# A transformer kernel on one core: where a feed-forward's down-projection tiles stand in the stream of weights

## The chip, the cores and the metric

The kernel runs on one core of one Trainium2 chip. The metric is the device time of one execution in microseconds (us). TensorE does the matrix products, VectorE and ScalarE the elementwise work, GpSimd (POOL) a few tiny operations, and SyncE (SP) issues the DMAs.

## What is computed

Two blocks of two layers each run on a sequence of 256 tokens with 1024 channels, in fp32: a convolution layer and an attention layer, each with a feed-forward, and then a retention layer and a sparse-attention layer. The change touches the feed-forward alone, which stands behind each layer of the first block:

```python
def conv_ffn(h, w_up, w_dw, b_dw, w_down):
    u = h @ w_up                       # (256, 1024) @ (1024, 5632)
    u = causal_dwconv(u, w_dw, b_dw)   # three taps over tokens, per channel
    gate, val = jnp.split(u, 2, axis=-1)
    return (jax.nn.silu(gate) * val) @ w_down   # (256, 2816) @ (2816, 1024)

x = x + conv_ffn(rmsnorm(x, g_ffn[l]), w_up[l], w_dw_f[l], b_dw_f[l], w_down[l])
```

## The kernel before

**Weights as a stream of tiles.** All weights pass through the core once, as a stream of tiles of 128 x 2048 fp32 (1 MB), in the order that `plan_tiles` writes down. For each tile SP loads RAW, ScalarE rounds it to a high part WH (L1216), VectorE subtracts to get the low part WL (L1595, called the split here), and TensorE multiplies. A product is three passes: high by high, low by high, high by low (L710 to L712). RAW, WH and WL each hold three tiles (`RING`). ScalarE rounds tile t when it is loaded and TensorE is done with tile t - 3 (`w_used`); SP loads into RAW when tile t - 3 is split.

**The order on each engine is written out by hand.** Each engine runs its instructions in the order of its own program. On ScalarE and VectorE, `upto_n(n)` stands where rounds and splits are to go: it rounds or splits all tiles up to number n + 2 that are not yet done.

**A feed-forward** (`ffn`) has 11 steps (`FSTEP`). Step s has a gate tile `("fg", l, s)` and a value tile `("fv", l, s)`, each of 256 hidden channels, and, `LAG` = 2 steps later, a down tile `("fd", l, s)` that multiplies the finished product of step s into four banks that hold the residual's increment. Steps 0 and 1 have no down tile. Behind step 10 the down tiles of steps 9 and 10 follow alone. A gate or value tile is 48 matmuls with 256 columns, a down tile 24 with 512. Between the entry of the feed-forward and its end the work of a step is:

- VectorE scales the gate tile out of its bank (L1656), and splits one tile (L1595). ScalarE applies the bias and the middle tap (L1323, twice), VectorE the other two (L1728 and L1732, twice each).
- ScalarE takes the tanh of the gate (L1327) and rounds the next tile (L1216).
- VectorE scales the value tile (L1656), splits a tile, finishes the sigmoid (L1724), and, behind ScalarE's L1323, applies the taps to the value (L1728, L1732).
- VectorE multiplies gate and value (L1736, called the product). From step 2 to step 9 a third tile is rounded (behind ScalarE's value part) and split (behind L1736).
- ScalarE copies the product to its high part MH (L1332), VectorE subtracts to get the low part ML (L1741). TensorE's down tile waits for this (`lo_done`).

Behind the last down tile VectorE adds the four banks to x (L1611), TensorE transposes x (L844), ScalarE squares it for the next norm (L1234) and writes the next layer's activations (L1248), VectorE their low part (L1624).

`plan_banks` writes down which PSUM bank each product uses and who gives it back; ring A has four banks for gate and value tiles, ring B four for the transposes and the down tiles.

Of the kernel before, what the change touches and what calls it, by code (L numbers as in the profile page):

```python
# [62 lines left out]
def plan_tiles():  # L63

    t = []
    for j in range(3):
        t += [("ca", j), ("cg", j)]
    t += [("qm", 0)]
    for l in range(2):
        t += [("mk", l), ("mv", l)]  # L70
    t += [("o0", c) for c in O0_ORDER]

    def ffn(l):
        out = []
        for s in range(FSTEP):
            out += [("fg", l, s), ("fv", l, s)] + [("fd", l, s - LAG)] * (s >= LAG)
        return out + [("fd", l, s) for s in range(FSTEP - LAG, FSTEP)]

    t += ffn(0)
    t += FOX_FIRST + FOX_LATER + [("o1", c) for c in range(4)]  # L80
    t += ffn(1)
    for h in range(RH):
        t += [("rq", h), ("rk", h)]
    for h in range(RH):
        t += [("rv", h, 0), ("rv", h, 1), ("rg", h, 0), ("rg", h, 1)]
    t += [("ro", c) for c in range(8)]
    t += [("pe", 0)] + [("pg0", c) for c in range(4)]
    for n in ("kc", "vc", "ks", "kw"):
        t += [(n, j) for j in range(2)]
    for n in ("vs", "vw"):  # L90
        t += [(n, j) for j in range(2)]
    t += [(n, j) for n in ("c1k", "c1v") for j in CMP_ORDER]
    for j in range(8):
        t += [("nq", j), ("ng", j)]
    t += [("no", c) for c in range(8)]
    t += [("pe", 1)] + [("pg1", c) for c in range(4)]
    return t
# [25 lines left out]
def plan_banks():  # L123
# [53 lines left out]
    def ffn(l, n):  # L177
        enter(n, ("fg", l, 0), ("fv", l, 0))
        for s in range(1, FSTEP):
            gemm(("fg", l, s), "dve")  # L180
            gemm(("fv", l, s), "dve")
            if s == LAG:
                acc(f"f{l}", ("fd", l, FSTEP - 1))

    gemm(("ca", 0), "dve")
    gemm(("cg", 0), "dve")
# [143 lines left out]
def program(nc, wstream, params, consts, ident_in, x_in, mem_in, xT_in, memT_in, p_in, b_f, g_final, final_norm, out):  # L330
    NT = len(TILES)
    with ExitStack() as ctx:
# [349 lines left out]
        def _(pe):  # L682
# [256 lines left out]
            def ffn(l, n, n_next):  # L939
                enter(n, (("fg", l, 0), XH, XL), (("fv", l, 0), XH, XL))  # L940
                for s in range(1, FSTEP + LAG):
                    if s < FSTEP:
                        gemm_t(("fg", l, s), XH, XL)
                        gemm_t(("fv", l, s), XH, XL)
                    if s == LAG:
                        o = [take((f"f{l}", q)) for q in range(4)]
                    if s >= LAG:
                        d = s - LAG
                        pe.wait_ge(*lo_a.next())
                        if d < FSTEP - 1:  # L950
                            gemm_d(("fd", l, d), o, MH, ML, 2 * (d % 4), d == 0)
                        else:
                            gemm_d_last(("fd", l, d), o, MH, ML, 2 * (d % 4), None, n_next)

            def ple(l):
                n = 7 + 2 * l
# [246 lines left out]
        def _(act):  # L1203
# [109 lines left out]

            def ffn(l):
                for s in range(FSTEP):
                    e, at = s % 2, TILE[("fg", l, s)]
                    for q, name in enumerate(("fg", "fv")):
                        upto_n(at + 1 + q)
                        is_free(act, (name, l, s))
                        for b in range(2):  # L1320
                            f = q * 22 + 2 * s + b
                            c = slice((2 * q + b) * T, (2 * q + b + 1) * T)
                            act_fn(fy[:, e, c], fu[:, e, c], ACT.Identity, bias=col(f"b_dw_f{l}", f),  # L1323
                                   scale=col(f"w_dw_f{l}", 2 * 44 + f)).then_inc(act_for_dve, 1)
                        if q == 0:
                            act.wait_ge(*dve_a.next())
                            act_fn(fth[:, e, :], fy[:, e, 0:2 * T], ACT.Tanh, scale=0.5).then_inc(act_for_dve, 1)  # L1327
                    if LAG <= s < FSTEP - 1:
                        upto_n(at + 3)
                    act.wait_ge(*dve_a.next())  # L1330
                    m = 2 * (s % 4)
                    act_fn(MH[:, m:m + 2, :], fa[:, e, :].rearrange("p (b t) -> p b t", b=2), ACT.Copy).then_inc(hi_done, 1)  # L1332
                    if s == FSTEP - 1:
                        upto_n(at + 3)

            def ple(l, key):
                n = 7 + 2 * l
# [245 lines left out]
        def _(dve):  # L1583
# [128 lines left out]

            def ffn(l):
                for s in range(FSTEP):
                    e, at = s % 2, TILE[("fg", l, s)]
                    y = fy[:, e, :].rearrange("p (b t) -> p b t", b=4)
                    u = fu[:, e, :].rearrange("p (b t) -> p b t", b=4)
                    for q, name in enumerate(("fg", "fv")):
                        scaled((name, l, s), u[:, 2 * q:2 * q + 2, :])
                        upto_n(at + 1 + q)  # L1720
                        is_free(dve, (name, l, s))
                        if q == 1:
                            dve.wait_ge(*act_a.next())
# [9 lines left out]
                        sync()  # L1733
                        if q == 0:
                            dve.drain().then_inc(dve_for_act, 1)
                    stt(fa[:, e, :], fth[:, e, :], 0.5, fy[:, e, 2 * T:4 * T], ALU.mult, ALU.mult).then_inc(dve_for_act, 1)  # L1736
                    if LAG <= s < FSTEP - 1:
                        upto_n(at + 3)
                    dve.wait_ge(*hi_a.next())
                    m = 2 * (s % 4)  # L1740
                    tt(ML[:, m:m + 2, :], fa[:, e, :].rearrange("p (b t) -> p b t", b=2),  # L1741
                       MH[:, m:m + 2, :].bitcast(F32), ALU.subtract).then_inc(lo_done, 1)
                    if s == FSTEP - 1:
                        upto_n(at + 3)

            def ple(l, acc, key):
                n = 7 + 2 * l
# [589 lines left out]
```

## Time and profile before

| | |
|---|---|
| median of 3 runs | 1295.65 us (1293.98 to 1296.0) |
| profiled execution | 1293.94 us, its span 1292.0 us |
| granted TensorE clock, mean | 0.985 |
| TensorE matmuls busy | 1244.0 us (96%) |
| TensorE weight loads busy | 1112.0 us (86%) |
| VectorE busy | 889.9 us (69%) |
| ScalarE busy | 640.1 us (50%) |
| POOL busy | 12.4 us (1%) |
| DMA | 200.54 MB, 155 GB/s |
| splits L1595 | 180, 2289 ns each |
| rounds L1216 | 180, 1910 ns each |

Busy time overlaps between engines, and that of TensorE is modelled from the starts of pipelined matmuls. A matmul's row is longer than the distance to the next one's start, so distances between starts are what to count with. The same holds for rows on VectorE and ScalarE, by some 0.1 us each. In a row, the part in square brackets is how long the engine stood idle before it and what ended that.

### The profile page before, as it was taken

What the parts mean: (1) busy time and instruction counts of PE and PEld (TensorE: products, weight loads), DVE (VectorE), ACT (ScalarE), POOL (GpSimd) and SP (SyncE); (2) the same over time, 40 slices, a digit from 0 to 9 for tenths busy, and PEclk for the clock granted to TensorE, in tenths of its full rate; (3) what the DMA queues carried; (4) which work ended last, traced back from release to release, by engine and by line L of the source; (5) the groups of instructions that cost most, each with busy time, mean ns of one, the idle gap of its engine ahead of it and who ended that gap; (6) DMA issues with size and microseconds to landing.
All of it is one profiled execution on the core that took longest, in us unless ns stands there. A gap on an engine that the chain in (4) does not pass through costs nothing.

```text
span 1292.0 us, 19500 instructions
## 1 busy us (share of the span) xinstructions
PE 1244.0 (96%) x8068; PEld 1112.0 (86%) x8068; DVE 889.9 (69%) x1358; ACT 640.1 (50%) x1015; POOL 12.4 (1%) x28
## 2 busy tenths in 40 slices
PE   6999899999999999999999999899899999999996
PEld 6988798999898769899999987687798989999885
DVE  5995678877755557887779666645485656666664
ACT  6563645555534335555555344425534545555453
POOL 0000000000000000000000000000000000000000
PEclk9999999999989999999999999999899899999998
DMA  9610445555342223455545544443355632222341
GB/s 387 233 66 5 160 166 193 199 193 188 139 155 106 99 98 131 156 211 188 195 164 176 191 155 185 165 160 131 133 196 195 228 109 97 98 99 98 130 169 60
DMA packets 28567, 200.54 MB, mean 155 GB/s; under 512 B 3392, under 2 KB 3520, under 8 KB 4928
## 3 DMA queue, kind: packets, MB, share of 16 engines
q1 hardware_dynamic: 28480, 199.30, 42.2%
q8 instruction: 64, 1.05, 0.3%
q14 instruction: 23, 0.19, 0.0%
HBM read 198.24 MB, written 1.05 MB: 154 GB/s over the span
## 4 chain that ended last, share of the span: by engine, by line
PE 82%; DVE 8%; issue 5%; ACT 4%; DMA 0%; DVEq 0%; POOL 0%; POOLq 0%; ACTq 0%; SPq 0%
PE bank L710 23%; PE bank L712 22%; PE bank L711 22%; PE bank L858 3%; DVE WL L1595 3%; ACT WH L1216 3%; PE bank L1190 1%; PE bank L1165 1%; PE bank L922 1%; PE bank L1156 1%; PE bank L1173 1%; PE bank L1188 1%; DVE work L1732 1%; DVE work L1728 1%; PE bank L914 1%
## 5 line engine op out<-in xcount | busy, mean ns | idle before, releaser
L1595 DVE TENSOR_TENSOR WL<-RAW,WH 128x2048 fp32r<-128x2048 f32 x180 | 411.6, 2289 | 173.7 <-ACT WH L1216 172.9
L1216 ACT ACTIVATE WH<-RAW 128x2048 fp32r<-128x2048 f32 x180 | 343.2, 1910 | 225.2 <-PE bank L712 221.7
L710 PE MATMUL bank<-XH,WH 128*128 128x256 f32 x1264 | 361.6, 286 | 17.9 <-DVE WL L1799 11.8
L711 PE MATMUL bank<-XL,WH 128*128 128x256 f32 x1264 | 358.2, 283 | 0.0
L712 PE MATMUL bank<-XH,WL 128*128 128x256 f32 x1264 | 358.0, 283 | 0.0
L710 PEld LDWEIGHTS bank<-XH,WH 128*128 128x128 f32 x1264 | 242.9, 192 | 22.4 <-DVE XL L1792 11.8
L711 PEld LDWEIGHTS bank<-XL,WH 128*128 128x128 f32 x1264 | 243.1, 192 | 0.5
L712 PEld LDWEIGHTS bank<-XH,WL 128*128 128x128 f32 x1264 | 243.0, 192 | 0.0
L710 PE MATMUL bank<-WH,MH 128*128 128x512 f32 (+1 forms) x544 | 202.5, 372 | 10.6 <-DVE work L2037 4.0
L712 PE MATMUL bank<-WH,ML 128*128 128x512 f32 (+1 forms) x544 | 199.9, 368 | 0.0
L711 PE MATMUL bank<-WL,MH 128*128 128x512 f32 (+1 forms) x544 | 199.8, 367 | 0.0
L710 PEld LDWEIGHTS bank<-WH,MH 128*128 128x128 f32 x544 | 105.9, 195 | 29.1 <-issue 5.6
L712 PEld LDWEIGHTS bank<-WH,ML 128*128 128x128 f32 x544 | 105.3, 194 | 16.3
L711 PEld LDWEIGHTS bank<-WL,MH 128*128 128x128 f32 x544 | 105.9, 195 | 14.6
L710 PE MATMUL bank<-WH,XH 128*128 128x512 f32 x192 | 76.3, 398 | 0.0
L711 PE MATMUL bank<-WL,XH 128*128 128x512 f32 x192 | 74.8, 390 | 0.0
L712 PE MATMUL bank<-WH,XL 128*128 128x512 f32 x192 | 74.7, 389 | 0.0
L710 PE MATMUL bank<-MH,WH 128*128 128x256 f32 x208 | 61.0, 293 | 4.4 <-DVE ML L1624 3.7
L1560 ACT ACTIVATE work<-bank,stat,rs_n 128x128 f32<-128x128 f32 (+1 forms) x96 | 42.9, 461 | 34.3 <-DVE stat L2153 34.3
L711 PE MATMUL bank<-ML,WH 128*128 128x256 f32 x208 | 59.7, 287 | 0.0
L712 PE MATMUL bank<-MH,WL 128*128 128x256 f32 x208 | 59.7, 287 | 0.0
L1323 ACT ACTIVATE work<-work,par 128x256 f32<-128x256 f32 x88 | 47.5, 587 | 4.8 <-DVE work L1656 4.8
(256 smaller groups left out, 1557.7 us busy)
## 6 DMA issues: line engine op xcount, KB each, us to landing
RAW<-wstream SPq DMA_DIRECT2D x181, 1024.0 KB, 4.8
con<-consts SPq DMA_DIRECT2D x1, 1681.0 KB, 13.5
work<-xT_in SPq DMA_DIRECT2D x1, 1024.0 KB, 4.8
x<-x_in SPq DMA_DIRECT2D x1, 1024.0 KB, 11.0
work<-mem_in SPq DMA_DIRECT2D x1, 1024.0 KB, 15.9
xn<-memT_in SPq DMA_DIRECT2D x1, 1024.0 KB, 13.7
out_dram<-xn SPq DMA_DIRECT2D x2, 512.0 KB, 2.7
par<-params SPq DMA_DIRECT2D x1, 858.0 KB, 14.2
```

Of the source, the lines that this page charges most:

```text
L710: mm(o, ah, bh, start=start, stop=False)
L711: mm(o, ah, bl, start=False, stop=False)
L712: return mm(o, al, bh, start=False, stop=stop)
L858: mm(conv_out[b][:, 0:T], diag[:, n % DIAGS, :], vpad[:, b, k:k + T], start=(k == 0), stop=last)\
L914: last = mm(o[:, i * T:(i + 1) * T], q_mem[r, h // 2, i * P:(i + 1) * P], mkt[r, l, h // 2, :], start=True, stop=True)
L922: mm(o[:, a:a + n], q1[r, h // 2, t], k1[r, h // 2, 0:n], start=True, stop=False)
L1156: mm(oS[:, a:a + n], qh[:, i * P:(i + 1) * P], ksT[:, g, 0:n], start=True, stop=False)
L1165: mm(oW[:, a:a + n], qh[:, i * P:(i + 1) * P], kwT[:, g, 0:n], start=True, stop=False)
L1216: act_fn(WH[:, t % RING, :], RAW[:, t % RING, :], ACT.Copy).then_inc(w_rounded, 1)
L1323: act_fn(fy[:, e, c], fu[:, e, c], ACT.Identity, bias=col(f"b_dw_f{l}", f), scale=col(f"w_dw_f{l}", 2 * 44 + f)).then_inc(act_for_dve, 1)
L1560: ins = act_fn(dst[:, e, b:b + w], B((name, s))[:, a:a + w], ACT.Exp, bias=stat[:, c:c + 1], scale=rs_n[:, i:i + 1], accum_out=stat[:, 16 ...
L1595: tt(WL[:, t % RING, :], RAW[:, t % RING, :], WH[:, t % RING, :].bitcast(F32), ALU.subtract).then_inc(w_split, 1)
```

## The change

In steps 2 to 9 the down tile moves from behind the value tile to a place between the gate and the value tile. Step 10 keeps the old order, and steps 0 and 1 have no down tile. The stream's order, the banks' plan, TensorE's program, and the places of the rounds and splits on ScalarE and VectorE all change with it: the round that stood behind ScalarE's value part now stands ahead of it, and on VectorE one split moves ahead of the scaling of the value and one behind it, ahead of the value's taps.

```diff
@@ plan_tiles
-            out += [("fg", l, s), ("fv", l, s)] + [("fd", l, s - LAG)] * (s >= LAG)
+            down = [("fd", l, s - LAG)] * (s >= LAG)
+            out += [("fg", l, s)] + (down + [("fv", l, s)] if s < FSTEP - 1 else [("fv", l, s)] + down)
@@ TensorE, ffn
                     if s < FSTEP:
                         gemm_t(("fg", l, s), XH, XL)
+                    if s == FSTEP - 1:
                         gemm_t(("fv", l, s), XH, XL)
...
                             gemm_d_last(("fd", l, d), o, MH, ML, 2 * (d % 4), None, n_next)
+                    if s < FSTEP - 1:
+                        gemm_t(("fv", l, s), XH, XL)
@@ ScalarE, ffn
                     for q, name in enumerate(("fg", "fv")):
-                        upto_n(at + 1 + q)
+                        upto_n(TILE[(name, l, s)] + 1)
...
                             act_fn(fth[:, e, :], fy[:, e, 0:2 * T], ACT.Tanh, scale=0.5).then_inc(act_for_dve, 1)
-                    if LAG <= s < FSTEP - 1:
-                        upto_n(at + 3)
+                            if LAG <= s < FSTEP - 1:
+                                upto_n(TILE[("fd", l, s - LAG)] + 1)
                     act.wait_ge(*dve_a.next())
@@ VectorE, ffn
                         scaled((name, l, s), u[:, 2 * q:2 * q + 2, :])
-                        upto_n(at + 1 + q)
+                        upto_n(TILE[(name, l, s)] + 1)
...
                         if q == 0:
                             dve.drain().then_inc(dve_for_act, 1)
+                            if LAG <= s < FSTEP - 1:
+                                upto_n(TILE[("fd", l, s - LAG)] + 1)
                     stt(fa[:, e, :], fth[:, e, :], 0.5, fy[:, e, 2 * T:4 * T], ALU.mult, ALU.mult).then_inc(dve_for_act, 1)
-                    if LAG <= s < FSTEP - 1:
-                        upto_n(at + 3)
                     dve.wait_ge(*hi_a.next())
```

The line numbers below L72 move by one to four in the changed kernel (the split L1595 becomes L1599, the product L1736 becomes L1742, the low part L1741 becomes L1745, the round L1216 becomes L1220).

VectorE, one step of the first feed-forward from the scaling of the gate to the low part, before:

```order
L1656 TENSOR_TENSOR work<-bank,rb 128x512
L1595 TENSOR_TENSOR WL<-RAW,WH 128x2048
L1728 SCALAR_TENSOR_TENSOR work<-work,par 128x255 x2
L1732 SCALAR_TENSOR_TENSOR work<-work,par 128x254 x2
L1656 TENSOR_TENSOR work<-bank,rb 128x512
L1595 TENSOR_TENSOR WL<-RAW,WH 128x2048
L1724 SCALAR_TENSOR_TENSOR work<-work 128x512
L1728 SCALAR_TENSOR_TENSOR work<-work,par 128x255 x2
L1732 SCALAR_TENSOR_TENSOR work<-work,par 128x254 x2
L1736 SCALAR_TENSOR_TENSOR work<-work 128x512
L1595 TENSOR_TENSOR WL<-RAW,WH 128x2048
L1741 TENSOR_TENSOR ML<-work,MH 128x512
```

VectorE, the same step of the changed kernel:

```order
L1660 TENSOR_TENSOR work<-bank,rb 128x512
L1599 TENSOR_TENSOR WL<-RAW,WH 128x2048
L1732 SCALAR_TENSOR_TENSOR work<-work,par 128x255 x2
L1736 SCALAR_TENSOR_TENSOR work<-work,par 128x254 x2
L1599 TENSOR_TENSOR WL<-RAW,WH 128x2048
L1660 TENSOR_TENSOR work<-bank,rb 128x512
L1599 TENSOR_TENSOR WL<-RAW,WH 128x2048
L1728 SCALAR_TENSOR_TENSOR work<-work 128x512
L1732 SCALAR_TENSOR_TENSOR work<-work,par 128x255 x2
L1736 SCALAR_TENSOR_TENSOR work<-work,par 128x254 x2
L1742 SCALAR_TENSOR_TENSOR work<-work 128x512
L1745 TENSOR_TENSOR ML<-work,MH 128x512
```

The second split went ahead of the scaling of the value, and the third from behind the product to behind that scaling; the product and the low part now follow each other.

ScalarE, one step of the first feed-forward from the round ahead of the gate's part to the high part, before:

```order
L1216 ACTIVATE WH<-RAW 128x2048
L1323 ACTIVATE work<-work,par 128x256 x2
L1327 ACTIVATE work<-work 128x512
L1216 ACTIVATE WH<-RAW 128x2048
L1323 ACTIVATE work<-work,par 128x256 x2
L1216 ACTIVATE WH<-RAW 128x2048
L1332 ACTIVATE MH<-work 128x512
```

ScalarE, the same step of the changed kernel:

```order
L1220 ACTIVATE WH<-RAW 128x2048
L1327 ACTIVATE work<-work,par 128x256 x2
L1331 ACTIVATE work<-work 128x512
L1220 ACTIVATE WH<-RAW 128x2048 x2
L1327 ACTIVATE work<-work,par 128x256 x2
L1336 ACTIVATE MH<-work 128x512
```

Both later rounds now stand in a row behind the tanh, ahead of the value's bias and middle tap.

## Rows read from the trace of the kernel before

**Rows 1.** Busy time by stretch: us long, then busy us of each engine (and instructions), PEclk, DMA share, GB/s.

```profile
217.84:302.74 84.90, 84.90 (x601) 80.11 (x600) 69.07 (x82) 46.64 (x48) 0.00 (x0) 1.00 0.54 193
```

**Rows 2.** Waits from 158 to 345 us: us in total, times, longest.

```profile
PE bank L710 <- DVE WL L1595: 2.0, 2, 1.4
```

**Rows 3.** Timeline, TensorE, first feed-forward: start, us, instruction, idle before.

```profile
200.01 0.36 PE L710 MATMUL bank<-XH,WH 128*128 128x256 f32 x1 [1.40 <-DVE WL L1595]
...
206.56 0.36 PE L710 MATMUL bank<-XH,WH 128*128 128x256 f32 x1 [0.56 <-DVE WL L1595]
...
212.38 0.40 PE L710 MATMUL bank<-WH,MH 128*128 128x512 f32 x1
...
217.84 0.28 PE L710 MATMUL bank<-XH,WH 128*128 128x256 f32 x1
...
234.82 0.28 PE L710 MATMUL bank<-XH,WH 128*128 128x256 f32 x1
...
342.14 0.39 PE L710 MATMUL bank<-WH,MH 128*128 128x512 f32 x1
```

**Rows 4.** Timeline, VectorE, steps 2 and 3 of the first feed-forward.

```profile
204.12 2.29 DVE L1595 TENSOR_TENSOR WL<-RAW,WH 128x2048 fp32r<-128x2048 f32 x1 [1.72 <-ACT WH L1216]
206.33 0.69 DVE L1724 SCALAR_TENSOR_TENSOR work<-work 128x512 f32<-128x512 f32 x1
206.93 0.88 DVE L1728 SCALAR_TENSOR_TENSOR work<-work,par 128x255 f32<-128x255 f32 x2
...
208.75 0.69 DVE L1736 SCALAR_TENSOR_TENSOR work<-work 128x512 f32<-128x512 f32 x1
209.36 2.28 DVE L1595 TENSOR_TENSOR WL<-RAW,WH 128x2048 fp32r<-128x2048 f32 x1
...
212.17 0.68 DVE L1656 TENSOR_TENSOR work<-bank,rb 128x512 f32<-128x512 f32 x1
212.77 2.28 DVE L1595 TENSOR_TENSOR WL<-RAW,WH 128x2048 fp32r<-128x2048 f32 x1
214.97 0.87 DVE L1728 SCALAR_TENSOR_TENSOR work<-work,par 128x255 f32<-128x255 f32 x2
...
219.30 2.29 DVE L1595 TENSOR_TENSOR WL<-RAW,WH 128x2048 fp32r<-128x2048 f32 x1 [1.72 <-ACT WH L1216]
```

**Rows 5.** Timeline, ScalarE, the same steps.

```profile
209.48 0.63 ACT L1332 ACTIVATE MH<-work 128x512 fp32r<-128x512 f32 x1 [2.60 <-DVE work L1736]
210.02 1.90 ACT L1216 ACTIVATE WH<-RAW 128x2048 fp32r<-128x2048 f32 x1
...
216.83 0.63 ACT L1327 ACTIVATE work<-work 128x512 f32<-128x512 f32 x1 [2.85 <-DVEq L1735]
217.37 1.90 ACT L1216 ACTIVATE WH<-RAW 128x2048 fp32r<-128x2048 f32 x1
```

**Rows 6.** Timeline, VectorE, last low part of both feed-forwards and what follows.

```profile
340.25 0.69 DVE L1741 TENSOR_TENSOR ML<-work,MH 128x512 fp32r<-128x512 f32 x1 [0.70 <-ACT MH L1332]
342.06 2.29 DVE L1595 TENSOR_TENSOR WL<-RAW,WH 128x2048 fp32r<-128x2048 f32 x1 [1.11 <-ACT WH L1216]
344.27 1.48 DVE L1611 TENSOR_TENSOR x<-bank,x 128x512 f32<-128x512 f32 x2
...
674.21 0.69 DVE L1741 TENSOR_TENSOR ML<-work,MH 128x512 fp32r<-128x512 f32 x1 [0.70 <-ACT MH L1332]
```

**Rows 7.** TensorE behind two long pauses, and the stretch behind each (columns as rows 1).

```profile
139.45 0.47 PE L710 MATMUL bank<-WH,MH 128*128 128x512 f32 x1 [3.13 <-DVE WL L1595]
139.45:143.00 3.55, 3.55 (x16) 2.94 (x17) 3.45 (x9) 1.85 (x2) 0.00 (x0) 1.00 0.67 240
...
840.31 0.47 PE L710 MATMUL bank<-WH,MH 128*128 128x512 f32 x1 [4.03 <-DVE work L2037]
...
840.30:844.60 4.30, 4.29 (x12) 3.43 (x13) 3.39 (x3) 0.00 (x0) 0.00 (x0) 0.60 0.00 0
```

**Rows 8.** DMA issues of the page: engine, operation, count, KB each, us to landing.

```profile
RAW<-wstream SPq DMA_DIRECT2D x181, 1024.0 KB, 4.8
```

More of the change, by code:

```diff
@@ L180, in ffn @@
             gemm(("fg", l, s), "dve")
-            gemm(("fv", l, s), "dve")
             if s == LAG:
                 acc(f"f{l}", ("fd", l, FSTEP - 1))
+            gemm(("fv", l, s), "dve")
     gemm(("ca", 0), "dve")
@@ L1315, in ffn @@
                 for s in range(FSTEP):
-                    e, at = s % 2, TILE[("fg", l, s)]
+                    e = s % 2
                     for q, name in enumerate(("fg", "fv")):
-                        upto_n(at + 1 + q)
+                        upto_n(TILE[(name, l, s)] + 1)
                         is_free(act, (name, l, s))
@@ L1714, in ffn @@
                 for s in range(FSTEP):
-                    e, at = s % 2, TILE[("fg", l, s)]
+                    e = s % 2
                     y = fy[:, e, :].rearrange("p (b t) -> p b t", b=4)
@@ L1735, in ffn @@
                             dve.drain().then_inc(dve_for_act, 1)
+                            if LAG <= s < FSTEP - 1:
+                                upto_n(TILE[("fd", l, s - LAG)] + 1)
                     stt(fa[:, e, :], fth[:, e, :], 0.5, fy[:, e, 2 * T:4 * T], ALU.mult, ALU.mult).then_inc(dve_for_act, 1)
-                    if LAG <= s < FSTEP - 1:
-                        upto_n(at + 3)
                     dve.wait_ge(*hi_a.next())
@@ L1743, in ffn @@
                     if s == FSTEP - 1:
-                        upto_n(at + 3)
+                        upto_n(TILE[("fd", l, s - LAG)] + 1)
             def ple(l, acc, key):
```

## The prediction

> **What bounds the kernel now.** I read the page first, then the busy time by stretch inside one feed-forward, then the waits there, and at last the instructions of single steps on TensorE, VectorE and ScalarE. Both feed-forwards give the same rows 334 us apart (340.25 and 674.21 for the last low part [rows 6]), so one is worked out and counted twice. The page's shares are means over a dozen stages and decide nothing here; the stretch does.
>
> In five full steps of the first feed-forward TensorE is busy for all of 84.90 us, its weight loads for 80.11, VectorE for 69.07 and ScalarE for 46.64 [rows 1]. The start of the gate tile of step 4 and that of step 5 are 16.98 us apart [rows 3]: that is TensorE's step, gate, value and down tile back to back, the down tile with 5.46 of it (212.38 to 217.84) and the other two with 5.76 each. So from there on TensorE bounds. Before that it does not quite: it waits twice for a split weight, 2.0 us together [rows 2], 1.40 before the gate tile of step 3 and 0.56 before its value tile [rows 3]. Steps 0 and 1 have no down tile, TensorE goes through them faster than the other two engines, and these come out of step 2 late.
>
> The question is how long the round that VectorE and ScalarE hand to each other takes. In the steps just after the start they are late and run as fast as they can. From the split at 204.12 to its counterpart at 219.30 it takes 15.18 us [rows 4]. That is 1.80 below TensorE's 16.98, so they make up their lateness step by step, and afterwards wait for TensorE. Some reserve of this sort is what the order of work in a step must keep.
>
> **What the change does to that round.** Nothing is added or removed: per step the same three splits (2.2 us each), rounds (1.9), taps and products, and on SP the same loads of 1 MB. A load lands 4.8 us after its issue [rows 8] and is issued when the tile three before it has been split. Even where splits now stand closest, one scaling apart, the copy in the ring that is filled next was freed a whole step earlier than it is rounded, so loads stay hidden. If that cover were gone, the price would be a part of 4.8 us a step. POOL does nothing in these stretches. The banks of the gate and value tiles are given back by scalings two steps back, which is no limit.
>
> What moves is the third split of a step. Before, it stands behind the product L1736, and while VectorE does it (from 209.36, 2.28 long), ScalarE copies the product (209.48) and rounds the next step's first tile (210.02 on) [rows 4, 5]. When VectorE has done the split, the low part and a scaling, that rounded tile is ready, and VectorE splits at 212.77 without a wait. In the changed order the third split stands between the scaling of the value and the value's taps, on the path to the product; and behind the product there is nothing left but the low part and a scaling, so that VectorE must wait for ScalarE's copy and round. The second split too stands ahead of the scaling instead of behind it, and the scaling no longer fills VectorE's wait for the tanh and the round behind it.
>
> The new round from product to product, each hand-over from a row [rows 4, 5]: product to ScalarE's copy 0.73 (208.75 to 209.48); to the round 0.54 (210.02); round to split 1.93 (217.37 to 219.30); split to taps 2.20 (212.77 to 214.97); through both pairs of taps to the tanh 1.86 (216.83); to the round 0.54 (217.37); to the split of the down tile 1.93 (219.30); to the scaling of the value 2.21 (as 204.12 to 206.33); to the split of the value tile's place 0.60; to L1724 2.21; to the value's taps 0.60; to the product 1.82 (206.93 to 208.75). **The sum is 17.17 us**, against 15.18 now and against TensorE's 16.98. The two engines can no longer catch up: they stay as late as they were at step 2, and lose another 0.19 a step.
>
> **When the last product is there.** Up to the split at 204.12 nothing changes: the first two steps have the same order, the tile that holds TensorE up at 200.01 is still the eighth of the stream, and its split stands where it stood. The second wait, at 206.56, falls to the down tile that now has this place. So the gain at these two waits is nothing. Then, in step 2, scaling, split, L1724, taps and product follow: 204.12 + 2.21 + 0.60 + 2.21 + 0.60 + 1.82 = 211.56 for the product, where it was at 208.75. Seven rounds of 17.17 bring the product of step 9 to 331.75. The last step has its old order, with no third split: 0.73 + 0.54 + 1.93 + 2.20 + 1.86 + 0.54 + 1.93 + 2.21 + 0.60 + 1.82 = 14.36, product at 346.11. Its high part (0.73 later, 0.63 long) and its low part (0.03 behind it, 0.69 long [rows 6]) are done at 348.19, and TensorE starts 0.15 behind what it waits for (split 204.12 + 2.29, start 206.56 [rows 3, 4]). So **the last down tile starts at 348.34**. It starts at 342.14 now [rows 3], with 1.2 us in hand behind the low part of 340.25 + 0.69 [rows 6]. The loss at this place is 6.20 us in each feed-forward. It shows as some 0.2 us of waiting at each of seven or eight down tiles, and as one pause of 5 us at the end: the product of step 8 is at 314.58, the split of step 10's value tile, the second of step 9, starts 9.73 behind it at 324.31 and TensorE on it at 326.75; 5.76 for it and 5.46 for each of two down tiles end at 343.4, 4.9 us before 348.34.
>
> **Behind the last down tile.** Now the split at 342.06 lies 1.81 behind the low part, since the round comes behind the high part, and VectorE's first residual add is at 344.27, 2.13 behind the start of the down tile [rows 6, 3]. Late by the new chain, low part at 347.50, split at 349.31, add at 351.51: 3.17 behind the tile's start. The second add ends at about 352.8, 4.46 behind it. The transposes that wait for it stand behind three quarters of the tile, 4.09 behind its start. So they slip by 0.5, ScalarE's squares by 1.0, and what feeds the next product by about 0.7. Bounds for this term: 0, if the later waits of that entry take it up, and 1.0.
>
> The pause costs more where the clock reacts. After a pause of 4.03 us at 840.31 the granted clock of the next 4.3 us was 0.60 of full, which is a part at 1.2 GHz among 2.4 [rows 7]; at 0.5 while halved, 0.60 over 4.30 us is 3.4 us at the lower level, and it costs half of that, 1.7 us. After a pause of 3.13 us at 139.45 the clock stayed at full [rows 7]. A pause of 5 us is nearer to the first, so I take 1.7; with TensorE slower, the second add is in time for the transposes, and the 0.7 is not counted beside it. The bounds are 0 and twice 1.7. The Trainium skill, TensorE: Matmul & The Clock Gate, What's actually happening, says that the throttled state is the default and that activity releases it; the trace agrees at 840.31, and by the rule alone any such pause is a risk of its own, beside the wait itself.
>
> **The sum.** 6.20 + 1.7 = 7.9 us per feed-forward, 15.8 for two. On the profiled execution's 1293.94 that is 1309.7; its time lies 1.7 under the median of the runs, 1295.65, and for the median I get **1311.5 us**.
>
> **Rivals.**
> (a) The same chain, but no loss of clock: 6.20 + 0.7 twice is 13.8, 1309.5 us. For it speaks the pause of 3.13 without one.
> (b) The round comes out shorter than TensorE's 16.98, because a hand-over overlaps that I put in a row (a second round behind the first is back to back on ScalarE, say). At 16.5 the two engines gain 0.5 a step and the last product is 8 times 0.67 = 5.4 earlier than in my chain; 2 times 0.8 and no clock loss, some 2 to 8 us in all, 1298 to 1304. Against it: each hand-over has its row, and the same way of adding gives exactly 15.18 for the present order.
> (c) No change, 1295.65: VectorE is busy 69.07 of 84.90 and has 16 us to spare [rows 1], TensorE stays full, and the lateness hides in the ring. The Trainium skill, Perfetto Trace Analysis, Identifying the Most-Contended Engine, has one look for the engine of the highest occupancy, weight loads for TensorE, and improve that; by it TensorE stays the bound and an order that leaves its work alone changes nothing. The trace agrees that TensorE is the fullest in this stretch. Against it: the limit here is a round through two engines, and it is 17.17 however idle each is.
> (d) Faster. The down tile of step 0, put ahead of the value tile, gives VectorE and ScalarE 5.5 us before the value is asked for, and the two waits of 1.40 and 0.56 go in both feed-forwards: 3.9 us, 1291.7. It decides itself at one point: whether the split of step 3's gate tile is done by 198.6, when TensorE comes to it. Against it: the same three tiles stand ahead of it on TensorE, and VectorE's order up to it is the same.
>
> **How the numbers follow.** My forecast has 0.60, (a) 0.25, (b) 0.06, (c) 0.05, (d) 0.04. The range: below, (a) without the 0.7 is 1308.1, and an error of 0.1 in the round (8 rounds, twice, 1.6) gives 1306.5; I go to 1304.5 to take in the nearest of (b). Above, another 1.7 of lost clock twice is 1314.9, and with 1.6 for the round 1316.5. So 1304.5 to 1317. A measurement of this kernel can tell about 0.2%, 2.6 us, from no change; faster by more than that is (d), 0.04; within it (c), 0.05; slower 0.91.
>
> **What would show it.** Right: a period of about 17.2 us between gate tiles; VectorE idle behind each low part, waiting for a round, and again ahead of the second split; splits of the second and third place one scaling apart; TensorE's wait for the low part (L1745) before the last down tile of each feed-forward, near 5 us, and two stretches of lower clock behind it. Wrong: a period of 16.98 with TensorE full, or the last down tile less than 3 us later than 342.14; then a term of the round overlaps. If the wait is there but the clock stays, (a) holds. If loads (L596) appear among what ScalarE's rounds wait for, my cover for the DMAs was wrong.

## The result

| | before | changed |
|---|---|---|
| median | 1295.66 us (4 runs, 1293.98 to 1296.0) | 1313.54 us (4 runs, 1312.47 to 1314.59) |
| ratio to before | | 1.0137 (95% interval 1.0122 to 1.0152) |
| span of the profiled execution | 1292.0 us | 1310.6 us |
| mean granted clock | 0.985 | 0.980 |

The changed kernel is slower by 17.9 us between the medians and by 18.6 between the profiled spans. The forecast was 1311.5 in a range of 1304.5 to 1317.

From the page of the changed kernel, the busy times of the engines (with instructions) and the shares of the chain that ended last:

```profile
PE 1253.2 (96%) x8068; PEld 1116.5 (85%) x8068; DVE 889.5 (68%) x1358; ACT 638.2 (49%) x1015; POOL 12.4 (1%) x28
...
PE 61%; DVE 21%; ACT 9%; issue 8%; DMA 0%; DVEq 0%; POOL 0%; ACTq 0%; POOLq 0%; SPq 0%
```

The shares of busy time tell nothing of it: VectorE and ScalarE do the same work in the same time. The chain does. Of the span before, 82% went over TensorE and 8% over VectorE; now it is 61% and 21%.

### The profile page after: what moved, and what is told of

It reads as the page before. It is cut to its first block, busy times and chain, and to the rows that moved or that the text cites. A ratio compares the mean times of both kernels' runs of the same rounds, so it can differ in the third digit from the quotient of the medians.

```text
span 1310.6 us, 19500 instructions
## 1 busy us (share of the span) xinstructions
PE 1253.2 (96%) x8068; PEld 1116.5 (85%) x8068; DVE 889.5 (68%) x1358; ACT 638.2 (49%) x1015; POOL 12.4 (1%) x28
## 4 chain that ended last, share of the span: by engine, by line
PE 61%; DVE 21%; ACT 9%; issue 8%; DMA 0%; DVEq 0%; POOL 0%; ACTq 0%; POOLq 0%; SPq 0%
PE bank L711 15%; PE bank L712 15%; PE bank L713 15%; DVE WL L1599 8%; ACT WH L1220 7%; DVE work L1736 3%; DVE work L1732 3%; PE bank L859 3%; PE bank L1194 1%; DVE work L1742 1%; DVE work L1660 1%; DVE work L1728 1%; PE bank L1169 1%; PE bank L923 1%; PE bank L1160 1%
## 5 line engine op out<-in xcount | busy, mean ns | idle before, releaser
L1599 DVE TENSOR_TENSOR WL<-RAW,WH 128x2048 fp32r<-128x2048 f32 x180 | 411.6, 2289 | 183.6 <-ACT WH L1220 182.8
L1220 ACT ACTIVATE WH<-RAW 128x2048 fp32r<-128x2048 f32 x180 | 341.0, 1908 | 183.8 <-PE bank L713 180.2
L711 PE MATMUL bank<-WH,MH 128*128 128x512 f32 (+1 forms) x544 | 206.8, 380 | 20.9 <-DVE ML L1745 9.2
L1336 ACT ACTIVATE MH<-work 128x512 fp32r<-128x512 f32 x22 | 13.9, 632 | 92.5 <-DVE work L1742 92.5
```

Source lines behind the costliest of these rows:

```text
L711: mm(o, ah, bh, start=start, stop=False)
L1220: act_fn(WH[:, t % RING, :], RAW[:, t % RING, :], ACT.Copy).then_inc(w_rounded, 1)
L1599: tt(WL[:, t % RING, :], RAW[:, t % RING, :], WH[:, t % RING, :].bitcast(F32), ALU.subtract).then_inc(w_split, 1)
```

## The profile after

**The round.** VectorE in steps 2 and 3 of the first feed-forward, the counterpart of [rows 4] (start, us, instruction, idle before):

```profile
204.32 2.29 DVE L1599 TENSOR_TENSOR WL<-RAW,WH 128x2048 fp32r<-128x2048 f32 x1 [2.55 <-ACT WH L1220]
206.53 0.68 DVE L1660 TENSOR_TENSOR work<-bank,rb 128x512 f32<-128x512 f32 x1
207.13 2.28 DVE L1599 TENSOR_TENSOR WL<-RAW,WH 128x2048 fp32r<-128x2048 f32 x1
209.33 0.68 DVE L1728 SCALAR_TENSOR_TENSOR work<-work 128x512 f32<-128x512 f32 x1
...
211.76 0.69 DVE L1742 SCALAR_TENSOR_TENSOR work<-work 128x512 f32<-128x512 f32 x1
213.15 0.69 DVE L1745 TENSOR_TENSOR ML<-work,MH 128x512 fp32r<-128x512 f32 x1 [0.70 <-ACT MH L1336]
213.75 0.68 DVE L1660 TENSOR_TENSOR work<-bank,rb 128x512 f32<-128x512 f32 x1
214.95 2.29 DVE L1599 TENSOR_TENSOR WL<-RAW,WH 128x2048 fp32r<-128x2048 f32 x1 [0.52 <-ACT WH L1220]
...
221.50 2.29 DVE L1599 TENSOR_TENSOR WL<-RAW,WH 128x2048 fp32r<-128x2048 f32 x1 [2.55 <-ACT WH L1220]
...
228.93 0.69 DVE L1742 SCALAR_TENSOR_TENSOR work<-work 128x512 f32<-128x512 f32 x1
```

ScalarE in the same steps, the counterpart of [rows 5]:

```profile
202.39 3.70 ACT L1220 ACTIVATE WH<-RAW 128x2048 fp32r<-128x2048 f32 x2
...
212.48 0.63 ACT L1336 ACTIVATE MH<-work 128x512 fp32r<-128x512 f32 x1 [4.13 <-DVE work L1742]
213.02 1.90 ACT L1220 ACTIVATE WH<-RAW 128x2048 fp32r<-128x2048 f32 x1
```

From product to product it is 228.93 - 211.76 = 17.17 us, which is the sum of the prediction to the second digit. The reader sees where it comes from: VectorE idle for 2.55 ahead of the second split, 0.70 ahead of the low part and 0.52 ahead of the first split, 3.77 in all. Before, in the same steps, only 1.72 stood ahead of the second split [rows 4]; the difference of 2.05 is, within the overlap of rows, the 1.99 us between the two rounds.

**TensorE.** The waits of TensorE between 158 and 350 us, and its rows behind the three of them (the counterparts of [rows 2, 3]):

```profile
PE bank L711 <- DVE ML L1745: 4.6, 1, 4.6
```

```profile
200.22 0.36 PE L711 MATMUL bank<-XH,WH 128*128 128x256 f32 x1 [1.40 <-DVE WL L1599]
...
206.76 0.47 PE L711 MATMUL bank<-WH,MH 128*128 128x512 f32 x1 [0.56 <-DVE WL L1599]
...
348.47 0.79 PE L711 MATMUL bank<-WH,MH 128*128 128x512 f32 x1 [4.61 <-DVE ML L1745]
```

The two waits of before are still there, 1.40 and 0.56, the second at a down tile now. The third, of 4.61, is new. The whole stage starts 0.22 later than in the trace of before (VectorE's copy L1638 at 167.48, L1634 at 167.26 before), so the last down tile, at 348.47 against 342.14, is late by 6.11 us; 6.20 was forecast.

A reader should note what the busy times of this stretch show, the counterpart of [rows 1]:

```profile
225.00:310.00 85.00, 85.00 (x598) 79.71 (x597) 65.67 (x80) 43.18 (x45) 0.00 (x0) 1.00 0.50 185
```

TensorE counts as busy for all of 85.00 us, though it waits 0.19 us in every step. A matmul's row is modelled longer than the distance to the next start, and such a gap lies inside it. No list of waits names it either. It shows in the period alone (17.17 for 16.98) and in weight loads that fall from 80.11 of 84.90 us [rows 1] to 79.71 of 85.00.

**Behind the pause.** VectorE at the last low part, the counterpart of [rows 6], and the granted clock behind the pause, the counterpart of [rows 7]:

```profile
347.73 0.69 DVE L1745 TENSOR_TENSOR ML<-work,MH 128x512 fp32r<-128x512 f32 x1 [0.69 <-ACT MH L1336]
349.53 2.29 DVE L1599 TENSOR_TENSOR WL<-RAW,WH 128x2048 fp32r<-128x2048 f32 x1 [1.11 <-ACT WH L1220]
351.74 0.68 DVE L1615 TENSOR_TENSOR x<-bank,x 128x512 f32<-128x512 f32 x1
353.64 0.69 DVE L1615 TENSOR_TENSOR x<-bank,x 128x512 f32<-128x512 f32 x1 [1.22 <-PE bank L713]
```

```profile
348.47:353.00 4.53, 4.53 (x11) 3.56 (x12) 2.89 (x2) 3.37 (x4) 0.00 (x0) 0.50 0.06 7
```

All of the 4.53 us behind the pause were at a granted clock of 0.50, that is at 1.2 GHz and not at 2.4. Half of that time is lost, 2.26. The clock had fallen within the pause already: it is 1.00 from 344.0 to 346.2 and 0.51 from 346.2 to 348.4. The second residual add waits 1.22 for TensorE, not the other way round, so the lateness of the adds is covered, as forecast. The next layer's first product starts at 358.07, and at 349.49 before: 8.36 later with the 0.22 taken off, 6.11 at the pause and 2.25 behind it. The second feed-forward repeats it, 6.1 and 2.6.

**What lies outside.** The two feed-forwards give 17.1 us, and 0.2 came ahead of them. The spans differ by 18.6. What is left goes with stretches of lower clock that fell differently. Before (first fence) and changed (second), stretches around the same work:

```profile
366.00:378.00 12.00, 12.00 (x65) 12.00 (x65) 3.14 (x6) 1.73 (x3) 0.00 (x0) 0.57 0.45 169
841.00:848.00 7.00, 7.00 (x26) 5.63 (x25) 2.69 (x2) 0.29 (x1) 0.00 (x0) 0.77 0.39 150
...
1040.00:1044.50 4.50, 2.84 (x24) 2.15 (x22) 1.67 (x3) 1.12 (x3) 0.00 (x0) 1.00 0.49 208
```

```profile
376.00:384.00 8.00, 8.00 (x44) 8.00 (x44) 1.72 (x6) 1.73 (x3) 0.00 (x0) 0.57 0.57 219
854.00:862.00 8.00, 6.11 (x15) 4.83 (x16) 5.24 (x5) 0.00 (x0) 0.00 (x0) 0.57 0.17 51
1059.00:1063.50 4.50, 4.14 (x20) 2.75 (x20) 0.34 (x1) 0.52 (x2) 0.00 (x0) 0.62 0.05 20
```

A stretch of 12 us at 0.57 is 10.3 us at the lower level, one of 8 us at 0.57 is 6.9. Behind the first feed-forward the changed kernel thus has 3.4 us less of it and gets 1.7 back; at the other two places it has some 3.5 us more each. From the next product behind the second feed-forward (15.59 late) to the end it loses another 3.0. This is added up from one trace of each kernel, and no run tests it. Such stretches also differ between executions of one kernel: at the place behind the first feed-forward e5 and e10, the same kernel, had 6.9 and 3.4 us of lower clock.

## The experiments

The theory under test: the tile order costs nothing by itself; what costs is where the second and third round and split stand in a step. They make the round through VectorE and ScalarE 17.17 us, over TensorE's 16.98, so that the lateness from steps 0 to 2 is never made up, and it is paid as one pause before the last down tile, with the clock on top. The rivals: the order of the tiles itself costs (the value tile of step 9 ends later, and the last product with it); each changed step costs its share; what is lost behind the pause is lost to late adds and not to the clock.

What every trace gave for the first feed-forward, as the start of the last down tile and of the next layer's first product, both counted from VectorE's copy L1634 (or its counterpart), less the same in the kernel before (174.88 and 182.23 us):

| run | last down tile | next product | ratio to before, 95% interval |
|---|---|---|---|
| changed | +6.11 | +8.36 | 1.0137 (1.0122 to 1.0152) |
| e1, new order, old places | +0.37 | +1.00 | 1.0019 (1.0006 to 1.0031) |
| e2, old order, new places | +6.14 | +9.06 | 1.0151 (1.0136 to 1.0166) |
| e3a, second split only | +1.04 | +1.04 | 1.0024 (1.0013 to 1.0034) |
| e3b, third split only | +1.73 | +2.36 | 1.0039 (1.0025 to 1.0052) |
| e4, steps 2 to 5 only | +0.78 | +0.77 | 1.0021 (1.0011 to 1.0030) |
| e7, pause filled | +6.10 | +6.73 | 1.0111 (1.0096 to 1.0125) |
| e8, the changed kernel again | +6.08 | +8.23 | 1.0143 (1.0128 to 1.0159) |
| e5, before with early round | -2.42 | -2.42 | 0.9973 (0.9961 to 0.9984) |
| e6, changed with early round | -1.49 | -0.86 | 0.9976 (0.9963 to 0.9990) |

### e1: the new order with the old places

```diff
@@ ScalarE and VectorE, ffn of the changed kernel
-                        upto_n(TILE[(name, l, s)] + 1)
+                        upto_n(TILE[(name, l, s)] + 1 - (q == 1 and LAG <= s < FSTEP - 1))
@@ ScalarE, behind the tanh; VectorE, behind the drain
-                            if LAG <= s < FSTEP - 1:
-                                upto_n(TILE[("fd", l, s - LAG)] + 1)
@@ ScalarE, behind the value part; VectorE, behind the product
+                    if LAG <= s < FSTEP - 1:
+                        upto_n(TILE[("fv", l, s)] + 1)
```

> The changed stream of tiles and TensorE program, but in steps 2 to 9 the second round and split stand behind the scaling of the value (split) and behind the tanh (round), and the third round behind the value part of ScalarE and the third split behind the product, as before the change. Theory (the places of the splits make the round 17.17 us): the round is 15.18 again, the pause before the last down tile shrinks to about 0.4 us, 1296 to 1298 us. Rival (the tile order itself costs, since the value tile of step 9 ends 5.5 us later and the last product with it): 1308 us or more, with a pause of several us before the last down tile.

Measured: 1299.13 us, ratio 1.0019. The median is 1.1 above the range expected; by the ratio to the executions of before that ran with it (median 1295.76) it is 1298.2, 0.2 above. The round from product to product is 15.19 (208.74 to 223.93). The pause of several us that the rival asks for is not there in TensorE's waits from 158 to 356 us:

```profile
PE bank L711 <- DVE WL L1599: 2.0, 2, 1.4
PE bank L711 <- DVE ML L1628: 1.4, 2, 0.8
PE bank L711 <- issue: 0.3, 1, 0.3
PE bank L845 <- DVE x L1615: 0.3, 1, 0.3
PE bank L711 <- DVE ML L1745: 0.2, 1, 0.2
```

The last line is all that is left of it (0.2 us as a row; 0.37 from start to start). So nearly all of the loss goes with the places. What stays, 1.0 us a feed-forward, is the order's own price, and it comes where the rival saw it: the value tile of step 9 ends a down tile later, and its product with it (e1, VectorE):

```profile
319.95 0.69 DVE L1660 TENSOR_TENSOR work<-bank,rb 128x512 f32<-128x512 f32 x1 [3.75 <-PE bank L713]
...
325.18 0.69 DVE L1740 SCALAR_TENSOR_TENSOR work<-work 128x512 f32<-128x512 f32 x1
```

Before, the same scaling was at 314.83 without a wait for TensorE, and the product at 321.88, 3.30 earlier. The last step makes up part of that, and the low part of step 10 is 1.50 late, against 1.2 in hand. The theory had nothing for this. Of the 1.0 us, 0.37 stands at the last down tile and 0.63 behind it, where the residual adds are late.

### e2: the old order with the new places

```diff
@@ ScalarE and VectorE, ffn of the kernel before
-                        upto_n(at + 1 + q)
+                        upto_n(at + 1 + q + (q == 1 and LAG <= s < FSTEP - 1))
@@ ScalarE, behind the tanh; VectorE, behind the drain
+                            if LAG <= s < FSTEP - 1:
+                                upto_n(at + 2)
@@ ScalarE, behind the value part; VectorE, behind the product
-                    if LAG <= s < FSTEP - 1:
-                        upto_n(at + 3)
```

> The stream of tiles and TensorE program of before, but in steps 2 to 9 the second and third round stand in a row behind the tanh, the second split ahead of the scaling of the value and the third ahead of its taps, as in the change. Theory: the round is 17.17 us and the last down tile starts 6.1 us late, with the pause and the loss of clock behind it: 1309 to 1315 us. Rival (tile order): within 2 us of before, 1295.7.

Measured: 1315.55 us, ratio 1.0151, 0.5 above the range expected. Two lines of TensorE's waits from 158 to 356 us:

```profile
PE bank L710 <- DVE ML L1741: 4.6, 1, 4.6
PE bank L710 <- DVE WL L1595: 2.0, 2, 1.4
```

The stream of before, with no tile moved, has the whole loss and the same pause of 4.6 us. Together with e1 this shows that the places are the cause, both ways round. Its last down tile is at +6.14, the changed kernel's at +6.11. It loses 2.92 behind the pause and not 2.25, with the clock at 0.50 for 5.98 us behind it (352.42 to 358.40) and not for 4.53.

### e3a and e3b: one split at a time

e3a puts the third split back behind the product, and ScalarE's third round behind its value part. e3b takes VectorE's second split out of its place behind the drain, so that it falls behind the scaling, with the third behind it:

```diff
@@ e3a: ScalarE and VectorE, ffn of the changed kernel
-                        upto_n(TILE[(name, l, s)] + 1)
+                        upto_n(TILE[(name, l, s)] + 1 - (q == 1 and LAG <= s < FSTEP - 1))
@@ e3a: ScalarE, behind the value part; VectorE, behind the product
+                    if LAG <= s < FSTEP - 1:
+                        upto_n(TILE[("fv", l, s)] + 1)
```

```diff
@@ e3b: VectorE, ffn of the changed kernel
                             dve.drain().then_inc(dve_for_act, 1)
-                            if LAG <= s < FSTEP - 1:
-                                upto_n(TILE[("fd", l, s - LAG)] + 1)
```

> The changed stream; only the second split stands ahead of the scaling of the value, the third again behind the product. Theory: the scaling no longer fills the wait for the round, so the round is 15.18 + 0.60 = 15.78 us, still under TensorE's 16.98: lateness is made up, one more wait of about 1 us at step 3: 1296.5 to 1299 us. Rival (each of the two moves alone costs half): 1304 us.

> The changed stream; only the third split stands ahead of the value's taps, the second again behind the scaling of the value. Theory: the round is 17.17 - 0.60 = 16.57 us, 0.41 under TensorE's step; the lateness is made up only in part, the last down tile starts 1.4 to 1.8 us late: 1298 to 1301 us. Rival (the third split on the path costs all of it): 1309 us or more.

Measured: e3a 1298.46 us, ratio 1.0024; e3b 1301.64, ratio 1.0039 (1300.8 by the ratio; the median is 0.6 above the range expected).

The time of e3a is as expected, its round is not. VectorE in steps 2 and 3, and in the last line ScalarE in step 2:

```profile
208.07 2.29 DVE L1601 TENSOR_TENSOR WL<-RAW,WH 128x2048 fp32r<-128x2048 f32 x1 [2.55 <-ACT WH L1220]
...
212.13 0.88 DVE L1734 SCALAR_TENSOR_TENSOR work<-work,par 128x255 f32<-128x255 f32 x2 [0.44 <-ACT work L1327]
...
224.50 2.29 DVE L1601 TENSOR_TENSOR WL<-RAW,WH 128x2048 fp32r<-128x2048 f32 x1 [2.55 <-ACT WH L1220]
...
211.00 1.09 ACT L1327 ACTIVATE work<-work,par 128x256 f32<-128x256 f32 x2 [2.96 <-DVE work L1662]
```

224.50 - 208.07 is 16.43 us, where 15.78 was expected. The expectation left out that the late scaling also holds up ScalarE's part of the value: ScalarE waits 2.96 for it, and VectorE's taps then wait for ScalarE, where nothing else is left to do. In the changed kernel the third split stands in that place and covers it. The 1.04 of e3a is a wait before the value tile of step 3, 0.80 as a row, as forecast.

VectorE's splits in e3b, in which the two pairs stand a round apart:

```profile
208.67 4.49 DVE L1599 TENSOR_TENSOR WL<-RAW,WH 128x2048 fp32r<-128x2048 f32 x2 [1.72 <-ACT WH L1220]
...
225.25 4.49 DVE L1599 TENSOR_TENSOR WL<-RAW,WH 128x2048 fp32r<-128x2048 f32 x2 [1.72 <-ACT WH L1220]
```

225.25 - 208.67 is 16.58 us, 16.57 was expected. The costs of the two moves do not add: 1.04 and 1.73 at the last down tile, 6.11 together. TensorE's step is the threshold. Each move alone leaves the round below 16.98 (16.43 and 16.58), and the lateness of VectorE and ScalarE shrinks by what is missing to it, step by step; both together, at 17.17, are above it.

### e4: the change in steps 2 to 5

With `HALF` = 6, steps 6 to 9 have the old order and the old places.

```diff
@@ plan_tiles
-            out += [("fg", l, s)] + (down + [("fv", l, s)] if s < FSTEP - 1 else [("fv", l, s)] + down)
+            out += [("fg", l, s)] + (down + [("fv", l, s)] if s < HALF else [("fv", l, s)] + down)
@@ ScalarE and VectorE, ffn (TensorE's tests in the same way)
-                            if LAG <= s < FSTEP - 1:
+                            if LAG <= s < HALF:
                                 upto_n(TILE[("fd", l, s - LAG)] + 1)
@@ ScalarE, behind the value part; VectorE, behind the product
+                    if HALF <= s < FSTEP - 1:
+                        upto_n(TILE[("fd", l, s - LAG)] + 1)
```

> The change in steps 2 to 5 only, steps 6 to 9 as before. Theory (a lateness that is no longer made up, and is paid once, before the last down tile): steps 6 to 9 make up 1.8 us each, no pause before the last down tile, only about 0.2 us of waiting in each changed step: 1296 to 1298.5 us. Rival (a cost per changed step): half of the loss, 1304 to 1305 us.

Measured: 1298.56 us, ratio 1.0021 (1.0011 to 1.0030). With half of the steps changed it has 2.7 of 17.9 us of the loss, and no wait for a low part before the last down tile. So the bulk of the loss is not per step: the last down tile is late by 0.78, four times the 0.19 by which the round exceeds TensorE's step. Steps 6 to 9 make the rest of the lateness up.

### e7 and e8: the pause filled, and the changed kernel again

```diff
@@ TensorE, ffn of the changed kernel
+                        if d == FSTEP - 1:
+                            is_free(pe, ("fg", l, FSTEP - 2))
+                            spare = B(("fg", l, FSTEP - 2))
+                            for _ in range(FILL):
+                                mm(spare[:, 0:T], XH[:, 0, 0:P], XH[:, 0, :], start=True, stop=True)
                         pe.wait_ge(*lo_a.next())
```

> The changed kernel; TensorE fills its pause before the last down tile of each feed-forward with 38 matmuls of 256 columns into a free bank, whose results nobody reads (38 x 0.12 = 4.6 us, the length of the pause). Theory (what is lost behind the pause is the clock's): the granted clock stays at full behind the pause, the 2.25 us lost behind each last down tile shrink to the 0.7 of the later residual adds or less: 1308 to 1311 us. Rival (it is lost to the later residual adds): as the changed kernel, 1313.5, or a little more.

> The changed kernel once more, beside the next one: 1312.4 to 1315 us. If the pause's loss of clock is what the filled pause gave back, its ratio stays above that of the filled pause (1.0111, at most 1.0125).

Measured: e7 1310.40 us, ratio 1.0111 (1.0096 to 1.0125); the changed kernel again 1315.03, ratio 1.0143 (1.0128 to 1.0159). These two intervals don't touch; that of the first measurement (1.0122 to 1.0152) overlaps with e7's by 0.0003, but the slowest of e7's four executions, 1310.78, is faster than the fastest of the changed kernel's eight, 1312.29. More work on TensorE makes the kernel 3 to 4 us faster. The granted clock of e7 around the last down tile (columns as rows 1):

```profile
343.00:349.00 6.00, 6.00 (x33) 5.18 (x32) 4.14 (x6) 3.42 (x4) 0.00 (x0) 1.00 0.40 158
348.50:353.00 4.50, 4.44 (x35) 4.20 (x35) 3.18 (x7) 1.91 (x2) 0.00 (x0) 1.00 0.61 233
353.00:358.00 5.00, 4.69 (x25) 3.68 (x25) 4.09 (x4) 3.81 (x7) 0.00 (x0) 1.00 0.20 39
```

It stays at 1.00, where the changed kernel was at 0.50. The last down tile starts at +6.10 as before, so the filling hides nothing of the lateness; the next product is 0.63 behind it instead of 2.25. So 1.6 us of the 2.25 is what the clock adds, and 0.63 is the price of the late adds that shows once the clock no longer covers it (0.7 was forecast for that case). The same 0.63 stands behind the last down tile of e1, e3b and e6, whose short waits before it cost no clock. In the second feed-forward the next product is at +6.77 in e7 and at +8.69 in the changed kernel, so the clock adds 1.9 there. The Trainium skill, TensorE: Matmul & The Clock Gate, What's actually happening, has activity release the throttle; the two runs agree with it.

### e5, e6, e9, e10, e11: a round ahead of the tanh

In every step ScalarE waits some 3 us for VectorE ahead of the tanh (2.85 in [rows 5]), does its second round behind it, and VectorE then waits 1.72 for that round [rows 4]. The round can go into that wait.

```diff
@@ ScalarE, ffn of the kernel before (e5; e9 has s < FSTEP - 1 for s <= LAG)
                         if q == 0:
+                            if s <= LAG:
+                                upto_n(at + 2)
                             act.wait_ge(*dve_a.next())
@@ ScalarE, ffn of the changed kernel (e6)
                         if q == 0:
+                            if s < FSTEP - 1:
+                                upto_n(TILE[(name, l, s)] + 2)
                             act.wait_ge(*dve_a.next())
```

> The kernel of before, with ScalarE's second round of steps 0, 1 and 2 ahead of the tanh instead of behind it, in time in which ScalarE waits for VectorE. Theory: the split no longer waits 1.72 us for it, the round through both engines is 1.7 shorter in these steps, the two waits of TensorE (1.40 and 0.56) go in both feed-forwards: 1291 to 1292.5 us. Rival (the round waits for TensorE there and holds the tanh up): no change or slower.

> The changed kernel, with ScalarE's second round of steps 0 to 9 ahead of the tanh. Theory: VectorE's wait of 2.55 us ahead of the second split goes, the round through both engines falls from 17.17 to about 14.6 us, no pause of several us before the last down tile (about 1 us): 1291.5 to 1294.5 us, faster than before. Rival (the tile order costs): over 1300.

Measured: e5 1292.36 us, ratio 0.9973; e6, the changed kernel with the same edit in steps 0 to 9, 1292.36, ratio 0.9976. In e5 both of TensorE's waits for a split are gone; VectorE in its step 1 (times of a trace that starts the stage 6.0 us later):

```profile
191.55 0.69 DVE L1658 TENSOR_TENSOR work<-bank,rb 128x512 f32<-128x512 f32 x1
192.16 2.28 DVE L1597 TENSOR_TENSOR WL<-RAW,WH 128x2048 fp32r<-128x2048 f32 x1
```

The split follows the scaling without the 1.72. In steps 1 and 2 of e5 the early round waits for nothing, in step 0 0.42 us for TensorE.

In e6 that one line on ScalarE turns a loss of 1.4% into a gain, with the changed tile order kept, which is the strongest form of what e1 says: the order costs little once the round is short. The round's own length of some 14.6, which was expected, can't be read off this trace: from product to product it takes 16.75 (205.51 to 222.26) and then TensorE's 16.98, and VectorE now waits for TensorE, 0.49 and 0.71 ahead of the scaling of the value. The new order still is not better than the old one: a pause of 0.8 us stays before the last down tile (-1.49 for -2.42), and the next product is at -0.86 for -2.42.

> The kernel of before, with the second round ahead of the tanh in steps 0 to 9 instead of 0 to 2. Theory (only the lateness of steps 0 to 2 costs TensorE anything, later steps are TensorE's): as with steps 0 to 2 alone, 1291 to 1292.5 us, the two waits gone. Rival (every shortened round helps): below 1290. Second rival (where ScalarE waits for TensorE ahead of the tanh, the product comes late): a wait before the last down tile, 1294 or more.

> The kernel of before with the early round in steps 0 to 2, once more, beside the one with it in steps 0 to 9. If both leave TensorE without a wait in the feed-forward, the two are equal within their intervals, at a ratio of 0.995 to 0.998.

> The early round in steps 0 to 9 once more. Equal to the one before within the intervals if the difference seen between them (0.9973 and 0.9953) is scatter; below it by 2 us again if the early round in steps 3 to 9 gives something of its own.

| run | median us | ratio to before, 95% interval |
|---|---|---|
| e5, steps 0 to 2 | 1292.36 | 0.9973 (0.9961 to 0.9984) |
| e9, steps 0 to 9 | 1290.55 | 0.9953 (0.9938 to 0.9968) |
| e10, steps 0 to 2 again | 1291.28 | 0.9956 (0.9939 to 0.9974) |
| e11, steps 0 to 9 again | 1292.49 | 0.9972 (0.9961 to 0.9983) |

The difference between the first two turned round when they were repeated. It is scatter: in the first feed-forward all four have the last down tile at -2.42 or -2.41, and TensorE waits for nothing in it. So steps 3 to 9 give nothing of their own. There TensorE is not yet done with the place that the early round writes to, as a row of e9 shows (ScalarE):

```profile
299.32 1.92 ACT L1216 ACTIVATE WH<-RAW 128x2048 fp32r<-128x2048 f32 x1 [2.86 <-PE bank L712]
```

The tanh follows it at 301.15 without a wait of its own, so the round now holds it up, but that costs TensorE nothing, so the second rival of e9 falls too. The median of e9, 1290.55, is 0.45 below the range expected. The kernel before with the early round, in steps 0 to 2 or in all, is faster than the kernel before by some 0.3 to 0.5%, and than the changed one by 1.6 to 1.9%. The medians can't tell it from e6 (0.9976, 0.9963 to 0.9990); the first feed-forward of the traces can, by 1.56 us at the next product.

## Why the prediction was right

- **The round of 17.17 us**, added up from hand-overs of the trace before: 17.17 measured. Waits of VectorE at the places named.
- **No gain at the two waits of steps 2 and 3**: both are there with their old lengths, 1.40 and 0.56, and the second has gone to a down tile. Rival (d) fell here.
- **The last down tile 6.20 us late**: 6.11. The pause, forecast at 4.9, was 4.61 for the matmuls and 5.0 for the weight loads. The 0.2 us of waiting in each step are in the period, but in no row and no list of waits.
- **Behind the pause 1.7 us**: this is the term that was mis-sized. It was taken from the stretch behind 840.31, where 3.4 us were at the lower level; here 4.53 us of work behind the pause were, and the price was 2.25 and 2.6. The bound of twice 1.7 held it. In e2 the same term was 2.92, nearer to that bound. That the clock is the reason for most of it, and rival (a) so not the case, is shown by e7. The pause of 3.13 us with a full clock, which spoke for (a), said little: behind its counterpart in e5, of 2.87, the clock was at 0.50. The late adds, which the sum did not count beside the clock, make 0.63 of it when the clock stays up.
- **The sum of 15.8 us**: 18.6 between the profiled spans, 17.9 between the medians. 1.5 of the difference is the term above. The rest, 3.0 lost late in the kernel and 1.7 gained behind the first feed-forward, is in stretches of lower clock far from the change, which the sum did not have. That they came to 1.3 us together, and not to 3 or more, is luck.
- **Rival (b)**, a hidden overlap in the round, had none. **Rival (c)**, TensorE as the fullest engine stays the bound, fell: it still counts as busy for 85.00 of 85.00 us, and the chain went to VectorE and ScalarE. The Trainium skill, Perfetto Trace Analysis, Identifying the Most-Contended Engine, has the engine of the highest occupancy optimized first. Read as rival (c) reads it, that gives no change here, and the measured 1.0137 decides against this reading.
- **Loads and POOL** were costed at nothing: no round waits for a load in the list of waits of this stretch, and TensorE's waits name no DMA.
- What I did not see is the order's own price. With short rounds, the value tile of step 9 ends a down tile later and the last product with it: 0.37 in e1, 0.8 of pause in e6. Under the long round it does not show: the old order has +6.14 in e2, the new one +6.11.
- The way of adding up hand-overs failed once, in e3a: 15.78 expected, 16.43 measured, because a wait of ScalarE for the later scaling was left out. In the changed kernel the third split covers that wait, so that its sum held.

## What to carry to other kernels

Where two engines hand work to each other in every step, add up the round from hand-over to hand-over and compare it with the bounding engine's step. The shares of busy time don't show it, and an edit costs little until the round passes that step: lengthened from 15.18 to 16.43 or 16.58 of 16.98 it cost 1.0 and 1.7 us before the last down tile, at 17.17 it cost 6.1, in a pause with a lower clock behind it. When an instruction moves, add up again the waits of every engine that its result feeds (e3a). Work that is only needed later, a round or a split, belongs into an engine's wait for the other, and not between two links of that round.

## What the runs showed of the hardware

- Filling a pause of TensorE with useless matmuls made the kernel faster, 1.0111 against 1.0143, because the granted clock stayed at 1.00 behind it, where it was 0.50 for 4.53 us.
- The mean granted clock and the time scatter between executions of one kernel: in e5 from 0.980 to 0.986, with 1288.76 to 1296.19 us, 7.4 apart. The stretches at 1.2 GHz scatter too: behind the first feed-forward 10.3 us in the kernel before and 6.9 in the changed one, but also 6.9 and 3.4 in e5 and e10, which are one kernel. Differences of 0.2% between kernels of this study need their traces, as in e9 to e11, and not their medians alone.
- The same pause can leave the clock up or not: behind 3.13 us at 139.45 it stayed at 1.00 [rows 7], while in e5 it was at 0.50 for at least 4.39 us behind the shorter wait at the same place of the program (columns of the last line as rows 1):

```profile
142.61 0.76 PE L710 MATMUL bank<-WH,MH 128*128 128x512 f32 x1 [2.87 <-DVE WL L1597]
...
142.61:147.00 4.39, 4.39 (x10) 3.44 (x11) 4.29 (x9) 1.85 (x2) 0.00 (x0) 0.50 0.83 256
```
